# Fetching the second expert table's tiles through a gather list that skips rows of zero weight

## The reference

```python
s1, i1 = lax.top_k(sc[:, :, 0], PEER_TOPK)          # 16 of 128 keys, twice, for each of 8 heads
s2, i2 = lax.top_k(sc[:, :, 1], PEER_TOPK)
cand_s = (s1[..., :, None] + s2[..., None, :]).reshape(PEER_CHUNK, PEER_HEADS, kk2)
cand_i = (i1[..., :, None] * PEER_N_KEYS + i2[..., None, :]).reshape(PEER_CHUNK, PEER_HEADS, kk2)
top_s, pos = lax.top_k(cand_s, PEER_TOPK)
idx = jnp.take_along_axis(cand_i, pos, axis=-1)     # 8 x 16 = 128 experts for each token
gate = jax.nn.softmax(top_s, axis=-1)
u = jnp.take(expert_u, idx, axis=0)
act = jax.nn.gelu(jnp.einsum('chkd,cd->chk', u, xc), approximate=False)
vsel = jnp.take(expert_v, idx, axis=0)
return jnp.einsum('chk,chkd->cd', (gate * act).astype(xc.dtype), vsel)
```

## Time and profile before

| | |
|---|---|
| Median of three runs | 4014.94 us (4009.41 to 4017.21) |
| The profiled execution | 4015.24 us, span 4013.4 us |
| PE busy | 3753.4 us, 94% |
| DVE / ACT / POOL busy | 57% / 11% / 24% |
| DMA | 1077.47 MB, mean 268 GB/s |
| V products, line 1747 | 1132.3 us busy, 38.8 us idle before them for tiles of the second table |
| U products, line 1674 | 1140.2 us busy, 20.3 us idle before them |

### The profile page before, as it was taken

One profiled execution on the slowest core, in us unless ns is written; L12 is line 12 of the kernel. 1 busy time (PEld: TensorE's weight loads), 2 busy tenths in 40 slices (PEclk: granted clock), 3 DMA queues, 4 the chain that ended last, 5 costly groups with the idle time before them and its releaser, 6 DMA issues. The chain is left out here.

```text
span 4013.4 us, 63920 instructions
## 1 busy us (share of the span) xinstructions
PE 3753.4 (94%) x26660; PEld 3401.8 (85%) x26660; DVE 2291.9 (57%) x4099; ACT 429.4 (11%) x1020; POOL 964.7 (24%) x868
## 2 busy tenths in 40 slices
PE   6997889999999999999879978899999999999997
PEld 5786774899999999999767867748999999999997
DVE  5965742785287544443469657517853875444434
ACT  1022210100111000000010232101001110000000
POOL 2610000034033333333225100000341333333331
PEclk9997899999999999999989978999999999999999
DMA  5430015399799999999744300154997999999997
GB/s 156 136 116 10 2 43 162 126 372 401 290 384 382 415 415 415 414 413 414 305 133 130 116 10 1 43 162 142 379 404 288 382 385 415 415 415 415 413 413 302
DMA packets 334770, 1077.47 MB, mean 268 GB/s; under 512 B 52196, under 2 KB 150872, under 8 KB 268440
## 3 DMA queue, kind: packets, MB, share of 16 engines
q1 hardware_dynamic: 223896, 670.72, 44.0%
q0 software_dynamic: 110592, 402.70, 25.3%
HBM read 1071.23 MB, written 2.10 MB: 267 GB/s over the span
## 5 line engine op out<-in xcount | busy, mean ns | idle before, releaser
L1747 PE MATMUL bank<-ex_W,ex_tile 128*128 128x160 f32 x8192 | 1132.3, 300 | 38.8 <-DMA ex_tile<-in_peer_v 38.8
L1747 PEld LDWEIGHTS bank<-ex_W,ex_tile 128*128 128x128 f32 x8192 | 1114.9, 190 | 59.7 <-DMA ex_tile<-in_peer_v 53.0
L1674 PE MATMUL bank<-ycT,ex_tile 128*128 128x160 f32 x8192 | 1140.2, 300 | 20.3 <-DMA ex_tile<-in_peer_uT 19.9
L1674 PEld LDWEIGHTS bank<-ycT,ex_tile 128*128 128x128 f32 x8192 | 1116.9, 190 | 36.0 <-DMA ex_tile<-in_peer_uT 30.4
L1631 POOL DMA_INDIRECT ex_row<-in_peer_u,ex_rows x384 | 403.5, 1051 | 1852.7 <-DVE ex_rows L1907 1187.4
L1943 DVE SCALAR_TENSOR_TENSOR ex_sums<-ex_row,ex_weight,ex_sums 128x2048 f32<-128x2048 f32 x186 | 436.9, 2349 | 412.9 <-DMA ex_row<-in_peer_v,ex_rows 412.8
L1937 DVE CUSTOM_DVE_ANT_0 ex_row<-ex_row,ex_h_wide 128x2048 f32<-128x2048 f32 x192 | 438.5, 2290 | 363.7 <-DMA ex_row<-in_peer_u,ex_rows 362.4
L1631 POOL DMA_INDIRECT ex_row<-in_peer_v,ex_rows x384 | 363.7, 947 | 878.9 <-DVE ex_sums L1943 565.7
L359 PE MATMUL pj_bank<-pj_hT,pj_piece 128*128 128x256 f32 x2048 | 458.7, 383 | 5.6 <-DMA pj_piece<-in_w_in 3.8
L359 PEld LDWEIGHTS pj_bank<-pj_hT,pj_piece 128*128 128x128 f32 x2048 | 387.9, 191 | 71.5 <-issue 13.8
L826 PE MATMUL bank<-arena,ycT 128*128 128x512 f32 x512 | 222.4, 593 | 2.0 <-PEq L911 2.0
(11 more groups left out here) (375 smaller groups left out, 3107.0 us busy)
## 6 DMA issues: line engine op xcount, KB each, us to landing
ex_tile<-in_peer_uT SPq DMA_DIRECT2D x256, 1024.0 KB, 8.1
ex_tile<-in_peer_v SPq DMA_DIRECT2D x256, 1024.0 KB, 8.2
pj_piece<-in_w_in SPq DMA_DIRECT2D x32, 2048.0 KB, 8.8
arena<-in_w_out SPq DMA_DIRECT2D x16, 2048.0 KB, 8.1
query_w<-in_peer_w_query SPq DMA_DIRECT2D x16, 1024.0 KB, 5.8
ex_row<-in_peer_u,ex_rows POOLq DMA_INDIRECT x384, 13.0
ex_row<-in_peer_v,ex_rows POOLq DMA_INDIRECT x384, 12.4
x<-in_x SPq DMA_DIRECT2D x1, 2048.0 KB, 8.9
```

Of the source, the lines that this page charges most:

```text
L1674: mm = mmul(o, ring[:, j % SLOTS, k * P:k * P + P], hT[k // 4][:, k % 4, 0:DENSE], start=(k == 0), stop=(k == KT - 1))
L1747: mm = mmul(bank[:, at_, lo:lo + DENSE], ring[:, i % SLOTS, m * P:m * P + P], W[:, j, :], start=(j == 0 and m % 3 == 0), stop=(j == TILES ...
```

## The change

SP no longer issues the V tiles; GpSimd does, in the same queue as the row sets, as one indirect gather of 128 rows of 8 KB each. Its list is a column of `ex_wanted`: for an expert with some weight that isn't zero, the row's number in the table; for one whose 160 weights are all zero, that number plus 65,536, which lies beyond the bound that the gather is given, so that the row is to be left out and the slot keeps what it held on that partition. VectorE makes the lists, eight tiles at a time (`want`), 13 of them after U tiles 104 to 116 and three after the last: a maximum of absolute values over 8 x 160 weights, a comparison with zero times 65,536, and an addition. GpSimd's order is now written out: row sets up to 86 (`rows_ahead(0)` is 87), then V tile 0, then one row set after each V tile until all 192 are issued, which is after tile 104. TensorE's products are the same, over all 128 rows. It waits for new semaphores `v_in`, one a slot, made outside the layer loop like `row_in`. The places of a widening and of the second set's folds are moved.

```diff
-WIDEN_2, FOLD_1, FOLD_1_AT = 36, 80, 152
+WIDEN_2, FOLD_1, FOLD_1_AT = 28, 64, 151
...
+    parts["lane"] = p
...
+        v_in = [sem(f"v_in{i}") for i in range(SLOTS)]
...
+NOWHERE = 65536.0
+CHUNK = 8
+
+def rows_ahead(j):
+    return min(served(TILES - SLOTS - 1) + RING - 1 + j, ROWS_IN)
...
+        weighty, expert = sb(st, "ex_weighty", [P, TILES]), sb(st, "ex_expert", [P, TILES])
+        wanted = sb(st, "ex_wanted", [P, TILES], U32)
...
+        v_rows = t["peer_v"].rearrange("l e d -> (l e) d")
...
-                def v_tile(i, slot, free):
-                    sp.wait_ge(tile_mm, free)
-                    sp.dma_start(ring[:, slot, :], t["peer_v"].rearrange("l (i e) d -> l i e d", e=KEYS)[layer, i])\
-                        .then_inc(tile_in[slot], 16)
...
-                ahead = SLOTS - TILES % SLOTS
-                for i in range(ahead):
-                    v_tile(i, (TILES + i) % SLOTS, TILES + i + 1 - SLOTS)
-                with sp.Fori(0, (TILES - ahead) // SLOTS) as lap:
-                    for e in range(SLOTS):
-                        v_tile(lap * SLOTS + (ahead + e), e, lap * SLOTS + (TILES + ahead + e + 1 - SLOTS))
-                for i in range(ahead + (TILES - ahead) // SLOTS * SLOTS, TILES):
-                    v_tile(i, (TILES + i) % SLOTS, TILES + i + 1 - SLOTS)
...
-                pool.wait_ge(rows_ready, SETS * 4 * 2)
-                for n in range(ROWS_IN):
+                def gather(n):
...
+                def v_tile(j):
+                    slot = (TILES + j) % SLOTS
+                    if j % CHUNK == 0:
+                        pool.wait_ge(index_ready, j // CHUNK + 1)
+                    pool.wait_ge(tile_mm, TILES + j + 1 - SLOTS)
+                    nc.gpsimd.indirect_dma_start(
+                        out=ring[:, slot, :], out_offset=None, in_=v_rows[:, :],
+                        in_offset=bass.IndirectOffsetOnAxis(ap=wanted[:, j:j + 1], axis=0),
+                        bounds_check=DEPTH * EXPERTS - 1, oob_is_err=False).then_inc(v_in[slot], 16)
+
+                pool.wait_ge(rows_ready, SETS * 4 * 2)
+                for n in range(rows_ahead(0)):
+                    gather(n)
+                for j in range(TILES):
+                    v_tile(j)
+                    for n in range(rows_ahead(j), rows_ahead(j + 1)):
+                        gather(n)
...
-                    pe.wait_ge(tile_in[i % SLOTS], 16 * (i // SLOTS + 1))
+                    pe.wait_ge(v_in[i % SLOTS], layer * (16 * ((TILES - 1 - j % SLOTS) // SLOTS + 1)) + 16 * (j // SLOTS + 1))
...
+                def want(i):
+                    some = slice(CHUNK * i, CHUNK * i + CHUNK)
+                    dve.wait_ge(gates_times, GROUPS)
+                    dve.wait_ge(tile_times, max(CHUNK * i + CHUNK - FIRST, 1))
+                    do(V.tensor_reduce(weighty[:, some], W[:, some, :], AX.X, ALU.max, apply_absolute_value=True))
+                    do(V.tensor_scalar(weighty[:, some], weighty[:, some], 0.0, NOWHERE, ALU.is_equal, ALU.mult))
+                    V.tensor_tensor(wanted[:, some], weighty[:, some], expert[:, some], ALU.add).then_inc(index_ready, 1)
...
+                do(V.tensor_scalar(expert[:], c("iota"), float(KEYS), c("lane"), ALU.mult, ALU.add))
+                do(V.tensor_scalar(expert[:], expert[:], layer_base[:], None, ALU.add))
...
+                    if 0 <= g - GROUPS < (FIRST + GROUPS) // CHUNK:
+                        want(g - GROUPS)
+                for i in range((FIRST + GROUPS) // CHUNK, TILES // CHUNK):
+                    want(i)
```

More of the change, by code:

```diff
@@ L195, in build @@
             route(nc, t, layer, sem, sb, bank, c, col, x, ycT, hT, query, out_w)
-            experts(nc, t, layer, sem, sb, bank, c, x, hT, query, W, low, layer_base, row_in)
+            experts(nc, t, layer, sem, sb, bank, c, x, hT, query, W, low, layer_base, row_in, v_in)
             rw.close()
@@ L1524, in _, with experts @@
                 do(V.reciprocal(rms[:, 2], rms[:, 1]))
+NOWHERE = 65536.0
+CHUNK = 8
+def rows_ahead(j):
+    return min(served(TILES - SLOTS - 1) + RING - 1 + j, ROWS_IN)
 def served(j):
     return BEFORE + max(j - FIRST + 1, 0) * 9 // 10
-def experts(nc, t, layer, sem, sb, bank, c, x, hT, query, W, low, layer_base, row_in):
+def experts(nc, t, layer, sem, sb, bank, c, x, hT, query, W, low, layer_base, row_in, v_in):
     q_mm, q_out, score_mm, score_out = [sem("ex_" + n) for n in ("q_mm", "q_out", "score_mm", "score_out")]
@@ L1548, in experts @@
                                                                                           "gelu", "sums")]
+    index_ready = sem("ex_index")
     wide_mm, wide_out, fold_mm, fold_added = [sem("ex_" + n) for n in ("wide_mm", "wide_out", "fold_mm", "fold_added")]
```

## The result

The changed kernel takes 4132.19 us (median of 4, 4126.63 to 4133.53) against 4016.07 us for the kernel before on the same chip: ratio 1.0289, 95% interval 1.0271 to 1.0307. The forecast was 3992 us, with a range of 3978 to 4050.

The account below looks back on a forecast made before the run. In the V halves PE and DMA limits coincide; only PE's idle 20.4 and 21.1 us can be won. With 9 left in each, 23.5 less 0.5 for lists and waits gives 23 us: 4015.2 to 3992 us, range 3978 to 4050.

Parts of the forecast that it names:

- The bytes that go: V tiles: 31% of rows have zero weight and move nothing; SP's queue falls by 268 MB, GpSimd's rises by about 185.
- Rival (c): V halves: a skipped row still moves bytes, 5.05 us a tile, 637 us a half, 4108 us in all; chance 0.08.
- The new rhythm: V half: tile plus row set are 1.77 MB, 4.27 us of DMA at 415 GB/s against PE's 4.44.
- GpSimd's queue: V half: three gathers a tile at 0.94 + 0.30 us take 3.72 of 4.44 us, leaving 0.7 to catch up.
- Rival (a): V half: unevenness or GpSimd's pace (8 KB row costing twice, 4.66 us a tile) eats the gain, 4015 us; chance 0.19.
- The rule that I weighed: VectorE in two-port mode locks GpSimd out; in a V half only the line-1940 steps (2.6 us) would hold a tile.
- The slack of 3.3 us: V tile: its slot is free 8.88 us ahead, issue and landing take 5.6 us, so 3.3 us absorb bad stretches.
- Unevenness: V half: the fullest DMA engine delays tiles; with the half's opening, fold and widening, 9 us of PE idle a half.
- VectorE's lists: First half, tiles 104 to 116: 1.9 us a list, reduction 1.48, fills VectorE's idle gap and costs nothing.
- Rival (b): V half: one queue instead of two, with an unoverlapped gap per transfer; at 0.15 us each, 4042 us; chance 0.20.
- Its sign: V half: DMA below 400 GB/s while PE waits would show that the single queue's gaps bind.
- The row sets' landing: V half: landing, 16.0 us in the saturated queue, falls to 8 to 10 us, so GpSimd's wait for places doesn't bind.

Follow-up runs that it names:

- experiment 1: Changed kernel with a list that leaves nothing out, so a tile brings 1.05 MB again: 4117.24 us, ratio 1.0234 to the kernel before.
- experiment 11: Changed kernel with one gather per row set (from set 87), one-operand VectorE sums and a fixed list even over DMA engines: 3964.7 us, ratio 0.9881.
- experiment 3: Changed kernel with each row set from set 87 on fetched by one gather of 8 KB rows instead of two of 4 KB: 4017.06 us, ratio 0.9985.
- experiment 2: Changed kernel with VectorE's two passes over a row set replaced by sums with one SBUF operand: 4038.88 us, ratio 1.0043.
- 10: Changed kernel with one gather per row set (from set 87) and VectorE's passes replaced by one-operand sums: 3977.36 us, ratio 0.9913.
- 7: Changed kernel with one gather per row set (from set 87) and a list that leaves nothing out: 4091.55 us, ratio 1.0175.
- 6: Changed kernel with one gather per row set (from set 87) and a fixed list, even over the DMA engines: 4004.46 us, ratio 0.9956.

## Why the prediction was wrong

The result lies beyond all the rivals, where a chance of 0.01 had been left.

**The bytes** ("The bytes that go") were right: 185.0 and 268.4 MB, and the left-out rows show as packets below 512 B (62,385 against 52,196, 10,189 more, and 10,191 rows were counted as unpicked). Rival (c), that a left-out row moves bytes, is false, although its 4108 us is the nearest of all to 4132. Its price was right for its case: 637 us a half (which makes 4106 or 4107, not 4108), measured 637.2 and 636.7 in experiment 1. A time that comes near is no proof of a mechanism.

**The new rhythm** of 4.27 us a tile was right as what DMA can do: experiment 11 stands at PE's floor.

**GpSimd's queue is the step that failed.** It said 3 x (0.94 + 0.30) = 3.72 us a tile, from a median of 937 ns. Measured: 5.21 us. The median was that of a kernel in which the end of VectorE's pass released the gathers, so the two seldom met (6 of 192); the change took this order away by putting GpSimd's work on TensorE's clock. The trace had the warning: the maximum of 2994 ns in the same row, which I left at "0.7 us a tile to catch up", and the 2.67 us of the earlier trace rows, which I put down to line 1992. That reading was wrong. The gather had begun 0.42 us into a pass of line 1937, and it ended 0.81 us after that pass:

```profile
1277.59 2.28 DVE L1937 CUSTOM_DVE_ANT_0 ex_row<-ex_row,ex_h_wide 128x2048 f32<-128x2048 f32 x1
```

Of the 32 gathers over 1.2 us in the whole trace of the kernel before, 26 began inside line 1937 and 4 inside line 1943, none inside line 1992. Lines 1937 and 1943 both read two SBUF operands. VectorE spends 2.3 us of each tile in such a pass, and a GpSimd that issues without a break meets nearly every one: 102 hold-ups beside 103 passes in 1400 to 1940 us. The hold-up costs 412.45 - 275.5 (96 tile gathers at 1.00, 191 halves at 0.94) = 137 us in 500, 1.4 us a tile. Rival (a) had the right engine, but neither the cause nor the price: a row that costs GpSimd twice, which the 937 ns of experiment 3 refute, and 0.22 us over PE's tile instead of 0.77.

**The rule that I weighed** was half read. The Trainium skill, SBUF — State Buffer (section SBUF: two separate sides), names beside the two-port modes also a VectorE instruction with two SBUF inputs, against a GpSimd instruction that reads SBUF. A gather reads its list there. The runs agree: long gathers beside the passes with two operands, none beside the sums with one (experiment 2), and none where no list is read (0 of 91). The half of the rule that I did use also held: the step of line 1940 does hold a gather (20 of 20), but a half has only two of them. Its other use, that the trace agreed on line 1992, was the wrong reading above.

**The slack of 3.3 us** took GpSimd as free when a slot is released. With three gathers a tile it is often inside a row set's two. Experiments 2 and 10 differ only in this third gather: 594.0 and 594.5 us against 578.2 and 572.9, some 19 us a half that the sum did not have. This third gather also makes the row sets' packets 4 KB and not 8; experiments 1 and 7, which differ in the same way with all bytes moved, stand 8 us a half apart, so not all of the 19 need be the slack.

**Unevenness** was 9 us a half with the rest; measured, 12 to 13 us for both layers (experiments 3 to 6, and 10 to 11). Right in size; how it falls on the two layers is not settled (0.7 and 8.8 us of the halves in the first pair, 10.2 and 3.0 in the second).

**VectorE's lists** cost nothing, as said. The first half takes 617 us as before, and the reduction 1.48 us in this row of the changed kernel (worked out: 1.48):

```profile
L1952 DVE TENSOR_REDUCE ex_weighty<-ex_W 128x8 f32<-128x1280 f32 x15 | 22.2, 1482 | 0.0
```

**Rival (b)**, one queue with a gap after each transfer, is out by experiment 1: 412 GB/s against 415 in two queues. Its sign, under 400 GB/s while PE waits, was there all the same: a sign that two causes share decides nothing. **The row sets' landing** did not bind, as said: 8 to 10 us expected, 6.6 measured as the median in the second half.

## What to carry to other kernels

A duration read from a trace holds for the neighbours that it had there. When a change lets an engine issue freely that used to be released by another, ask what the two will now do at the same time, and look at the maximum and at the few long ones, not at the median. Where GpSimd must gather beside VectorE's two-operand passes and issues without a break, count one held gather for each pass, issue few and large gathers, or cut the passes into pieces. And when a long instruction is put down to a neighbour, check that the neighbour was running when it began.

## What was not expected of the hardware

A gather with a list in SBUF that begins inside a VectorE instruction with two SBUF operands ends 0.81 to 0.88 us after that instruction in the changed kernel; a TENSOR_SCALAR over 2048 elements, with one SBUF operand, does the same, while a TENSOR_REDUCE with one, and a TENSOR_TENSOR with one in SBUF and one in PSUM, hold nothing. A plain transfer from the same queue took 0.53 to 0.58 us beside the same passes. 128 rows cost GpSimd 0.94 to 1.00 us, be they 4 or 8 KB. And in a full DMA that two queues share, one gather of 8 KB rows for a row set instead of two of 4 KB rows took the tiles' part of the bytes from 55% to 51%, which was worth 1.9% of the kernel's time.
